# Weighted one-hots of the late chunks made on GpSimd by compare-and-scale operations of one token each, in place of a VectorE comparison and GpSimd products of two tokens

## What is computed

```
idx = i_top * 128 + j_top                      # 8 heads x 16 slots a token
g   = softmax(best)
act = gelu(einsum('thkd,td->thk', u_tab[idx], xb))
out = einsum('thk,thkd->td', g * act, v_tab[idx])
```

## Time and profile before

| what | value |
|---|---|
| median of 3 runs | 2246.83 us (2246.06 to 2248.22) |
| the profiled execution, its own time | 2247.59 us |
| span in its trace | 2245.8 us |
| late chunks of layer 0 | about 530 to 800 us |
| late chunks of layer 1 | about 1612 to 1873 us |
| TensorE busy | 93% of the span |
| VectorE, ScalarE, GpSimd busy | 71%, 59%, 43% |

### The profile page before, as it was taken

One profiled execution on the slowest core, in us unless ns is written; L12 is line 12 of the kernel. 1 busy time (PEld: TensorE's weight loads), 2 busy tenths in 40 slices (PEclk: granted clock), 3 DMA queues, 4 the chain that ended last, 5 costly groups with the idle time before them and its releaser, 6 DMA issues.

```text
span 2245.8 us, 42297 instructions
## 1 busy us (share of the span) xinstructions
PE 2094.1 (93%) x14238; PEld 1844.4 (82%) x14238; DVE 1603.4 (71%) x2994; ACT 1334.3 (59%) x2370; POOL 963.5 (43%) x818
## 2 busy tenths in 40 slices
PE   4998899999999999999989579898999999999998
PEld 1777898989999987777769479898999998777776
DVE  1446565796888878777867453949799998877785
ACT  1444443456777767667744534455777776766774
POOL 1010027777888732223300000888777773222330
PEclk7999999999999999999999889999999999999999
DMA  7753536666555568888844344454533446888883
GB/s 268 267 190 126 177 114 225 235 225 222 190 182 196 198 228 297 296 305 293 294 154 141 107 134 131 133 177 153 198 127 130 131 131 203 302 299 302 294 293 126
DMA packets 125618, 459.89 MB, mean 205 GB/s; under 512 B 14144, under 2 KB 14672, under 8 KB 124480
## 3 DMA queue, kind: packets, MB, share of 16 engines
q1 hardware_dynamic: 103104, 377.14, 49.8%
q0 software_dynamic: 21504, 79.53, 9.6%
q10 hardware_dynamic: 896, 1.76, 0.2%
HBM read 449.93 MB, written 8.44 MB: 204 GB/s over the span
## 4 chain that ended last, share of the span: by engine, by line
PE 74%; DVE 8%; issue 6%; POOL 6%; ACT 3%; DMA 3%; POOLq 0%; ACTq 0%; DVEq 0%; SPq 0%
PE pm L1264 11%; PE pm L1266 11%; PE pm L1265 10%; PE pu L1194 7%; PE pu L1189 7%; PE pu L1190 6%; PE pu L1062 4%; POOL w_lo L506 3%; PE pu L1064 3%; PE pu L1063 3%; PE pm L1224 2%; PE pm L1225 2%; POOL w_lo L545 1%; PE pm L1084 1%; PE pu L1509 1%
## 5 line engine op out<-in xcount | busy, mean ns | idle before, releaser
L1566 DVE TENSOR_TENSOR w_lo<-raw,w_hi 128x1024 fp32r<-128x1024 f32 x492 | 627.3, 1275 | 418.2 <-ACT w_hi L660 367.9
L660 ACT ACTIVATE w_hi<-raw 128x1024 fp32r<-128x1024 f32 x604 | 637.5, 1056 | 445.0 <-PE pm L1266 225.2
L1189 PE MATMUL pu<-hid_hi,w_hi 128*128 128x256 f32 x2048 | 504.9, 287 | 8.4 <-ACT w_hi L660 8.4
L1190 PE MATMUL pu<-hid_lo,w_hi 128*128 128x256 f32 x2048 | 496.2, 281 | 0.0
L1189 PEld LDWEIGHTS pu<-hid_hi,w_hi 128*128 128x128 f32 x2048 | 388.8, 190 | 34.3 <-issue 31.0
L1264 PE MATMUL pm<-w_hi,hid_lo 128*128 128x512 f32 x1024 | 403.6, 394 | 2.2 <-DVE hid_lo L1807 2.2
L1266 PE MATMUL pm<-w_lo,hid_lo 128*128 128x512 f32 x1024 | 402.4, 393 | 0.0
L1265 PE MATMUL pm<-w_hi,hid_lo 128*128 128x512 f32 x1024 | 401.6, 392 | 0.0
L1190 PEld LDWEIGHTS pu<-hid_lo,w_hi 128*128 128x128 f32 x2048 | 388.6, 190 | 0.0
L506 POOL TENSOR_TENSOR w_lo<-raw,w_hi 128x1024 fp32r<-128x1024 f32 x112 | 299.8, 2687 | 201.0 <-ACT w_hi L660 200.2
L1194 PE MATMUL pu<-hid_hi,w_lo 128*128 128x256 f32 x2048 | 294.6, 286 | 16.3 <-POOL w_lo L506 15.7
(11 more groups left out here) (272 smaller groups left out, 3091.0 us busy)
## 6 DMA issues: line engine op xcount, KB each, us to landing
raw<-in_u_tab SPq DMA_DIRECT2D x256, 512.0 KB
raw<-in_v_tab SPq DMA_DIRECT2D x256, 512.0 KB
raw<-in_ada SPq DMA_DIRECT2D x96, 512.0 KB
raw<-in_wq SPq DMA_DIRECT2D x32, 512.0 KB
raw<-in_gla_in SPq DMA_DIRECT2D x24, 512.0 KB
raw<-in_rg_in SPq DMA_DIRECT2D x20, 512.0 KB
arena<-in_gla_state POOLq DMA_DIRECT2D x8, 512.0 KB, 10.4
raw<-in_gla_out SPq DMA_DIRECT2D x8, 512.0 KB
```

What stands on the lines that cost most here:

```text
L660: act.activation(w_hi[:, s2, :], raw[:, s4, :], ACT.Copy).then_inc(hi_done, 1)
L1189: mm(pu[:, s, 0:SEQ], w_hi[:, s % 2, kk * P:kk * P + P], hid_hi[:, kk, 0:SEQ], start=(kk == 0), stop=False)
L1190: mm(pu[:, s, 0:SEQ], w_hi[:, s % 2, kk * P:kk * P + P], hid_lo[:, kk, 0:SEQ], start=False, stop=False)
L1566: tt_(w_lo[:, s2 if l2 is None else l2, :], raw[:, s4, :], w_hi[:, s2, :].bitcast(F32), ALU.subtract).then_inc(lo_done, 1)
```

## The change

`first_hot` and its buffer `oh_eq` and its semaphore `eq_ready` go. GpSimd makes each weighted one-hot itself out of the ramp `iota`, the slot's i (`sel_i`) and the slot's weight (`sel_w`), by one operation with two per-partition operands: (iota == i) * weight. Each operation covers one token and one part (high or low), so a group needs four operations of 128 x 128 in place of two of 128 x 256. The GpSimd loop over groups is written out.

```
@@
-        oh_eq = sb("oh_eq", [P, 2, 2, NKEY], BF16)
@@
                 def firsts(i, first):
                     for r in range(2):
-                        pool.wait_ge(eq_ready, i * 2 + (g0 + r + 1))
                         if lay or not first:
                             pool.wait_ge(oh_used, i * 2 + (g0 + r - 1))
-                        w_h = sel_w[:, 0, bass.ds(i * 4 + r * 2, 2)].bitcast(F32).unsqueeze(2).to_broadcast([P, 2, NKEY])
-                        w_l = sel_w[:, 1, bass.ds(i * 4 + r * 2, 2)].bitcast(F32).unsqueeze(2).to_broadcast([P, 2, NKEY])
-                        pool.tensor_tensor(oh_hi[:, r], oh_eq[:, r], w_h, ALU.mult)
-                        pool.tensor_tensor(oh_lo[:, r], oh_eq[:, r], w_l, ALU.mult).then_inc(oh_ready, 1)
+                        for t in range(2):
+                            at = slice(4 * i + 2 * r + t, 4 * i + 2 * r + t + 1)
+                            for part, dst in enumerate((oh_hi, oh_lo)):
+                                last = pool.tensor_scalar(dst[:, r, t, :], iota, sel_i[:, 0, at],
+                                                          sel_w[:, part, at].bitcast(F32), ALU.is_equal, ALU.mult)
+                        last.then_inc(oh_ready, 1)
 
                 firsts(0, True)
-                with pool.Fori(1, GROUPS // 2) as i:
+                for i in range(1, GROUPS // 2):
                     firsts(i, False)
@@
-                def first_hot(i, g, r):
-
-                    tt_(oh_eq[:, r], numbers, sel_i[:, 0, bass.ds(i * 16 + 2 * g, 2)].unsqueeze(2).to_broadcast([P, 2, NKEY]),
-                        ALU.is_equal).then_inc(eq_ready, 1)
-
@@
-                    for r in range(2):
-                        if not final:
-                            dve.wait_ge(oh_ready, i * 8 + (g0 + 2 * s + r + 1))
-                            first_hot(i, 2 * s + r + 2, r)
@@
-                for r in range(2):
-                    first_hot(0, r, r)
```

More of the change, by code:

```diff
@@ L19 @@
 U32 = mybir.dt.uint32
-BF16 = mybir.dt.bfloat16
 ALU = mybir.AluOpType
@@ L349, in build_step @@
         (key_in, s_ready, s_evac, shift_ready, exp_ready, slot_ready, slot_t, sel_ready, oh_ready, oh_used,
-         eq_ready, ob_act, ob_vec, abs_done, w_made, wh_ready, w_ready, lo_pool, ada_row_ready, ada_tr, mod_ready,
+         ob_act, ob_vec, abs_done, w_made, wh_ready, w_ready, lo_pool, ada_row_ready, ada_tr, mod_ready,
          out_ready, outs_done) = [sem(n) for n in (
             "key_in", "s_ready", "s_evac", "shift_ready", "exp_ready", "slot_ready", "slot_t", "sel_ready",
-            "oh_ready", "oh_used", "eq_ready", "ob_act", "ob_vec", "abs_done", "w_made", "wh_ready",
+            "oh_ready", "oh_used", "ob_act", "ob_vec", "abs_done", "w_made", "wh_ready",
             "w_ready", "lo_pool", "ada_row_ready", "ada_tr", "mod_ready", "out_ready", "outs_done")]
```

## The result

The changed kernel takes 2607.73 us (median; 2605.55 to 2610.46) against 2247.02 us before: a ratio of 1.1606, 95% interval 1.1585 to 1.1626. It is 361 us slower. The forecast had the sign, but the time lies far above its range (2223 to 2440). The profiled execution took 2609.44 us with a span of 2607.6.

A forecast was written before the change was run, and what follows sets the result against it. TensorE bounds the kernel, but GpSimd's late chunk would grow to 8 x 0.42 + 1.17 = 4.53 us and set the beat: +22.0 us in layer 0, +28.5 in layer 1, together +50.5, giving 2298 us (range 2223 to 2440).

The forecast's parts named there:

- What bounds the kernel: TensorE, busy 93% of the span; only its gaps can be won, at most 23.2 us in layer 1's late chunks.
- Nothing to win: Late chunks of layer 0: TensorE is busy 130.27 of 131 us, so no gain is possible there.
- The beat: Late chunks: each interval becomes the larger of GpSimd's 4.53 us chunk and its own; GpSimd is at most one chunk ahead.
- Part 2: GpSimd's products become 8 x 128 x 128 a chunk, compare and multiply in one, at 0.42 us each.
- Part 3: Hold-ups of GpSimd by VectorE that stay: `low` 0.99 and `second_hot` 0.18, together 1.17 us a chunk.
- a further 0.01 us: Added to each GpSimd operation: 10 us once the chunk is above 4.5 us, about 6 us between 4.0 and that.
- a smaller hold-up: Late chunks: the forecast is wrong if `low` holds GpSimd up under 0.99 us because the operations are shorter.
- The other sign: Late chunks: the forecast is wrong if GpSimd stalls between instructions in the written-out program; no size given.
- Part 1: 256 comparisons leave VectorE, 119.6 us of busy time; VectorE is not the bound, so by themselves they give nothing.
- Part 4: GpSimd's loop written out: no register work between groups; what it gives lies inside idle time that goes anyway.
- The dear case: New GpSimd operation as dear as the present one: 0.61 us, chunk 6.05 us, +242 us, 2489 us; chance 0.18.
- The first rival: GpSimd becomes cheaper, below 0.35 us an operation; layer 1 gets TensorE's beat, up to 23.2 us less, 2224 us; chance 0.31.

The follow-up runs named there:

- after_add: The changed kernel with add in place of the compare in all 1024 fused GpSimd operations: 2306.76 us, ratio 1.0269.
- forms: The kernel before with rows of unread GpSimd operations put into its idle start; only its trace is used: compare and multiply of 128 columns took 0.770 us.
- no_eq: The kernel before with the GpSimd loop written out and VectorE's comparisons left out except in each layer's first chunk: 2227.61 us, ratio 0.9916.
- loop4: The kernel before with its GpSimd hardware loop over eight groups (four chunks) in place of two: 2235.09 us, ratio 0.9947.

## Why the prediction was right or wrong, by its steps

**What bounds the kernel** held in the main. Of the at most 23.2 us of layer 1 the written-out loop won 15.2, and no run brought its late intervals below 241.6 us, where 63 x 3.71 is 233.7. "Nothing to win" in layer 0 was not quite right: the loop won 2.9 us there, in intervals of 4.05 to 4.23 that a TensorE busy for 130.27 of 131 us didn't show.

**The beat** held as a mechanism: with GpSimd's chunk above TensorE's, the common late interval is GpSimd's own list and nothing else (6.81 = 8 x 0.773 + 0.62), TensorE waits for the weighted one-hots, and GpSimd can't save up. `after_add` is nearly the test of my own sum, since its operation costs 0.43 where I had taken 0.42: it took 2306.8 us against my 2298. Its chunks are 4.55 us in layer 1, where I had 4.53, and 4.67 in layer 0. The agreement is partly luck, since the hold-ups in it are not the ones that I had added up.

**Part 2, the price of the new operation, is the step that failed.** I took 0.42 us; it is 0.773 from start to start (0.787 long). The two bounds were rows of other kinds of operation. The nearest row, the copy of 0.349, was itself taken beside a `TENSOR_TENSOR` of VectorE (119.84, 1.35 us), which can have held it up; in `forms` a copy is 0.28 us long and 0.240 from start to start. So the copy was likely read too dear, and what stands between a copy and the new operation was taken far too cheap. The upper one, the product of 256 columns at 0.61, was no bound at all: I gave it as one because it reads four times as much, and by `forms` the largest single part of this operation is not in what it reads. 0.347 us are the compare against an add, and no row of the trace before had a compare on GpSimd. The two operands are 0.16. By the widths 0.34 us of the whole are fixed, and the change pays that eight times a chunk. The term mis-sized: 8 x (0.773 - 0.42) = 2.82 us a chunk, over 126 intervals 356 us too little. Part 3's error, 126 x (1.17 - 0.62), took 69 of it back. My 50.5 and these two make 337.

The measured loss in the intervals is 354.9, and the 17 between are intervals above 6.81: most of layer 0's are 6.80 to 6.82 with some up to 7.56, layer 1's mostly 6.8 to 7.4 with a few from 6.24 to 8.05 (440.5 - 63 x 6.81 = 11.5 us, and 5.7 in layer 0). The timelines account for these 17 us. GpSimd works through, and the operation that `low` holds up is between 1.40 and 1.88 us long in place of 1.41 throughout. `low` starts 0.03 to 0.14 us after TensorE's u_low ends, so any shift of u_low against GpSimd's operations changes what `low` takes. In the 36 chunks whose u_low took over 1.3 us (up to 2.02, at the lower granted clock) the held-up operation lasted 1.64 us on average in layer 0 and 1.68 in layer 1, against 1.42 and 1.49 in the others. So the lower clock goes with a part of the 17 us; no run held it fixed.

One step of the sum was also off by itself: between a chunk of 4.0 and one of 4.47 a further 0.01 us costs 0.08 x (24 + 63) = 7 us or more, not 6.

**Part 3, the blocks**, was 1.17 and came out at 0.62 in the changed kernel: `low` overlapped with an operation in flight, and `second_hot` cost nothing that shows. With the add it is 0.99, as the rows said. The prediction had named a smaller hold-up as a sign of being wrong, but tied it to shorter operations; here it came with longer ones. The other sign, stalls in the written-out program, did not come: 7.0 us of idle time before 1024 operations.

**Part 1** held: 122.6 us less on VectorE, and worth nothing measurable by itself (`no_eq`).

**Part 4, the written-out loop at nothing, was wrong**: alone it gives 18 us. I had put its work into GpSimd's idle time "that goes anyway"; the run shows that the long intervals of layer 1 depended on that work. Through which order of waits is argued and not shown. In the changed kernel the gain can't show, since GpSimd is never ahead. Against the written-out kernel the fused operations cost 2607.7 - 2229.2 = 378.5 us.

**The rivals.** The dear case came nearest: it had two steps of arithmetic and operands fetched apart, of which the runs show the compare (0.347) and the operands (0.16). But it stopped at 0.61 and 2489 us, below what was measured. The first rival's condition, below 0.35 us, fails by a factor of two. What so cheap an operation would have won no run shows; the runs that eased the hand-over in other ways stopped at 14 to 20 us.

## What to carry to other kernels

An operation that the trace doesn't hold is not bounded by a dearer-looking operation of another kind: its price can lie in a step of arithmetic, here a compare. When the whole forecast turns on that price, the range must go beyond the dearest neighbour, above all where the engine is already at the beat of its consumer. Fusing two operations into one was no gain here, because GpSimd pays for each instruction and for each step, and splitting the tiles to get per-partition operands doubled the number of instructions. A row taken for a price must be looked at for what ran beside it. And a loop written out in passing is an edit of its own: cost it, and test it alone.

## What the runs showed of the hardware that was not expected

- GpSimd, 128 partitions, start to start: compare and multiply with two per-partition operands 0.553, 0.770 and 1.200 us for 64, 128 and 256 columns; add and multiply 0.423 for 128; compare and multiply with two constants 0.61 for 128; compare alone 0.582; copy 0.240; product of two tiles 0.413 (`forms`). VectorE's comparison of 256 columns took 0.41 us at the shortest, 0.426 in the median.
- What VectorE's `low` (two inputs, 1024 columns, 1.22 to 1.37 us) takes from GpSimd depends on the operation in flight, which runs on beside it; the next one ends 0.65 to 0.68 us after `low` in 117 of 126 chunks of the changed kernel. The loss was 0.62 us where the one in flight had 0.54 of 0.79 to go, 1.01 where it had 0.11, and 0.99 in `after_add` where it had 0.12 of 0.44.
- A GpSimd hardware loop with one chunk in its body cost 18 us over two layers against the same list written out, and with four chunks in its body some 5 to 6 us. How its delays tip the order between `low` and GpSimd's four operations from one pattern into the other I read from the timelines; no run varied that order by itself, so it is argued and not shown. That the jump costs more than the register work rests on one run, `loop4`, and the split between the two stays open.
